# Differential attention: each unit's two weight tiles turned by products with diagonals of their factors and added in PSUM

## What is computed

```python
def diff_softmax_core(q, k, v, lam):
    s = jnp.einsum('bqhcd,bkhcd->bhcqk', q.astype(jnp.float32), k.astype(jnp.float32)) * (DA_HD ** -0.5)
    p = jax.nn.softmax(s, axis=-1)
    w = p[:, :, 0] - lam * p[:, :, 1]
    return jnp.einsum('bhqk,bkhe->bqhe', w, v.astype(jnp.float32))
...
    ax = diff_attn_latent(qx, jnp.concatenate([kc, kx], axis=1), jnp.concatenate([vc, vx], axis=1), lam)
...
    out_c = merge(diff_softmax_core(qc, kc, vc, lam), mc, pc[5]) if need_ctx else None
```

## Time and profile before

| | before |
|---|---|
| median of 3 runs | 2934.42 us |
| lowest, highest | 2933.34, 2937.86 us |
| the profiled execution's own time | 2933.31 us |
| its span, first to last instruction | 2931.3 us |
| outside the span | 2.0 us |
| mean granted TensorE clock | 0.983 |
| TensorE busy | 2828.8 us, 97% |
| VectorE busy | 2013.9 us, 69% |
| ScalarE busy | 1281.7 us, 44% |
| GpSimd busy | 339.3 us, 12% |
| chain that ended last | PE 80%, DVE 11%, ACT 5% |

### The profile page before, as it was taken

One profiled execution on the slowest core, in us unless ns is written; L12 is line 12 of the kernel. 1 busy time (PEld: TensorE's weight loads), 2 busy tenths in 40 slices (PEclk: granted clock), 3 DMA queues, 4 the chain that ended last, 5 costly groups with the idle time before them and its releaser, 6 DMA issues.

```text
span 2931.3 us, 44027 instructions
## 1 busy us (share of the span) xinstructions
PE 2828.8 (97%) x17694; PEld 2492.6 (85%) x17694; DVE 2013.9 (69%) x3397; ACT 1281.7 (44%) x2121; POOL 339.3 (12%) x380
## 2 busy tenths in 40 slices
PE   7999999998999999999999989999999999999998
PEld 6888898666888889888897889999979999887898
DVE  7789956555687656788655775666656689767764
ACT  4222244354422224222245565565455554645653
POOL 0000011322100001000011110022102210300100
PEclk8999999899999999999999999999999999999999
DMA  6666522011455534556432234455425579653453
GB/s 245 222 223 230 201 85 94 29 51 43 145 201 208 212 125 158 201 205 210 145 113 80 72 130 151 149 176 174 164 81 172 187 277 327 199 155 101 137 187 115
DMA packets 141194, 467.63 MB, mean 160 GB/s; under 512 B 27024, under 2 KB 29200, under 8 KB 140480
## 3 DMA queue, kind: packets, MB, share of 16 engines
q1 hardware_dynamic: 125440, 408.20, 41.2%
q0 software_dynamic: 15552, 56.63, 5.5%
HBM read 463.73 MB, written 1.05 MB: 159 GB/s over the span
## 4 chain that ended last, share of the span: by engine, by line
PE 80%; DVE 11%; ACT 5%; issue 2%; DMA 2%; POOL 1%; SPq 0%; ACTq 0%; DVEq 0%; POOLq 0%
PE bank L2657 24%; PE bank L2658 24%; PE bank L2659 24%; DVE sb_split_low L2061 3%; DVE sb_h_low L2148 1%; DMA sb_raw<-weights 1%; PE bank L2929 1%; PE bank L3100 1%; PE bank L2948 1%; DMA sb_ada_mlp<-ada 1%; DVE sb_temp L2075 1%; PE bank L2889 1%; DVE sb_x_res L2264 1%; DVE sb_temp L2142 1%; ACT sb_temp L1966 1%
## 5 line engine op out<-in xcount | busy, mean ns | idle before, releaser
L2657 PE MATMUL bank<-sb_h_high,sb_split_high 128*128 128x256 f32 (+1 forms) x3464 | 1116.6, 322 | 39.5 <-DVE sb_h_low L2156 16.5
L2658 PE MATMUL bank<-sb_h_low,sb_split_high 128*128 128x256 f32 (+1 forms) x3464 | 1097.8, 317 | 0.0
L2659 PE MATMUL bank<-sb_h_high,sb_split_low 128*128 128x256 f32 (+1 forms) x3464 | 1097.1, 317 | 0.0
L1646 ACT ACTIVATE sb_split_high<-sb_raw 128x1024 fp32r<-128x1024 f32 x620 | 646.4, 1051 | 306.6 <-PE bank L2659 286.2
L2061 DVE TENSOR_TENSOR sb_split_low<-sb_raw,sb_split_high 128x1024 fp32r<-128x1024 f32 x620 | 758.6, 1232 | 21.6 <-ACT sb_split_high L1646 21.5
L2657 PEld LDWEIGHTS bank<-sb_h_high,sb_split_high 128*128 128x128 f32 x3464 | 666.7, 192 | 100.9 <-issue 17.7
L2658 PEld LDWEIGHTS bank<-sb_h_low,sb_split_high 128*128 128x128 f32 x3464 | 667.8, 193 | 40.8
L2659 PEld LDWEIGHTS bank<-sb_h_high,sb_split_low 128*128 128x128 f32 x3464 | 667.0, 193 | 40.7
L2075 DVE CUSTOM_DVE_ANT_0 sb_temp<-sb_ada_ffn,sb_cond_ffn 128x1024 bf16<-128x1024 f32 x364 | 429.7, 1220 | 25.1 <-DMA sb_ada_ffn<-ada 16.0
L2657 PE MATMUL bank<-sb_hidden_high_ffn,sb_split_high 128*128 128x512 f32 (+1 forms) x830 | 280.4, 338 | 0.0
L2659 PE MATMUL bank<-sb_hidden_high_ffn,sb_split_low 128*128 128x512 f32 (+1 forms) x830 | 279.2, 336 | 0.0
(11 more groups left out here) (329 smaller groups left out, 3498.2 us busy)
## 6 DMA issues: line engine op xcount, KB each, us to landing
sb_raw<-weights SPq DMA_DIRECT2D x620, 512.0 KB, 3.4
sb_ada_ffn<-ada SPq DMA_DIRECT2D x114, 512.0 KB, 4.6
sb_ada_ffn<-ada POOLq DMA_DIRECT2D x90, 512.0 KB, 3.8
sb_ada_mlp<-ada POOLq DMA_DIRECT2D x18, 512.0 KB, 5.6
sb_ada_mlp<-ada SPq DMA_DIRECT2D x18, 512.0 KB, 5.9
sb_cond_ffn<-cond SPq DMA_DIRECT2D x3, 1024.0 KB, 5.4
sb_na_raw<-na_rpb SPq DMA_DIRECT2D x32, 96.0 KB, 6.8
sb_x_res<-tokens SPq DMA_DIRECT2D x4, 512.0 KB, 7.7
```

Of the source, the lines that this page charges most:

```text
L1646: do.activation(m.high[s % HIGHS][:, :], m.raw[s % RAWS][:, :], identity).then_inc(*act.mark("split_high", s))
L2657: do.matmul(out, ah, bh, start=start and j == 0, stop=False)
L2658: do.matmul(out, ah, bl, start=False, stop=False)
L2659: last = do.matmul(out, al, bh, start=False, stop=stop and j == len(terms) - 1)
```

## The change

`da_combine` is taken out of the list of steps, and `da_normalise` out of GpSimd's program. After the two factors, VectorE writes two diagonal matrices, the identity times factor 1 and the identity times factor 2, into two of six 128x128 places in `masks`. `da_turn` no longer transposes a combined tile: for each 128 keys it multiplies the first tile with the first diagonal and the second tile with the second one, and the two products are added in bank 3.

```diff
-    units = list(apart(turns(16, ("da_scores", "da_normalise", "da_combine", "da_turn"), more), "da_scores"))
+    units = list(apart(turns(16, ("da_scores", "da_normalise", None, "da_turn"), more), "da_scores"))
...
+    def da_diag(self, u, c):
+        at = (2 * (u % 3) + c) * P
+        return self.masks[:, at:at + P]
...
-    def da_normalise(u):
-        pool.wait_ge("exped", ("da", u, 1))
-        pool.wait_ge("recip", ("da", u))
-        first_scaled("da", u, m.cols[u % 6][:, 4:5])
...
         do.tensor_tensor(col[:, 5:6], col[:, 5:6], m.neg_lam[:, 0:1], ALU.mult).then_inc(*dve.mark("recip", ("da", u)))
+        dve.wait_ge("recip", ("da", u))
+        if u >= 3:
+            dve.wait_ge("turned", ("da", u - 3))
+        for c in range(2):
+            do.tensor_scalar(m.da_diag(u, c), m.C("ident"), col[:, 4 + c:5 + c], None, ALU.mult).then_inc(
+                *dve.mark("weights", ("da", u, c)))
...
-    def da_combine(u):
-        combine("da", u, m.cols[u % 6][:, 5:6])
...
     def da_turn(u):
-        pe.wait_ge("combined", ("da", u))
-        turn("da", u, 3, m.temp[2 * (u % 3)], even_keys(u))
+        nk = even_keys(u) // P
+        free(3)
+        for c in range(2):
+            pe.wait_ge("exped", ("da", u, c))
+            pe.wait_ge("weights", ("da", u, c))
+        for kt in range(nk):
+            for c in range(2):
+                last = do.matmul(m.bank[3][:, kt * P:(kt + 1) * P], m.temp[2 * (u % 3) + c][:, kt * P:(kt + 1) * P], m.da_diag(u, c),
+                                 start=c == 0, stop=c == 1)
+        last.then_inc(*pe.mark("turned", ("da", u)))
+        read[3] = "turn_copy", ("da", u)
```

More of the change, by code:

```diff
@@ L1591, in pool_program @@
     work = {"ada": ada, "square": square, "add_mean": add_mean, "centre": centre, "near_centre": near_centre,
-            "rope": rope, "da_normalise": da_normalise, "ml_normalise": ml_normalise, "even_norm": even_norm,
+            "rope": rope, "ml_normalise": ml_normalise, "even_norm": even_norm,
             "gla_decay3": gla_decay3, "gla_factors": gla_factors, "plain": plain}
@@ L2616, in vector_program @@
             "hidden_low": hidden_low, "add": add, "fm_copy": fm, "tm_copy": tm, "forget": forget, "lambda": lam,
-            "rope": rope, "conv": conv, "da_scores": da_scores, "da_normalise": da_normalise, "da_combine": da_combine,
+            "rope": rope, "conv": conv, "da_scores": da_scores, "da_normalise": da_normalise,
             "ml_weights": ml_weights, "ml_normalise": ml_normalise, "ml_combine": ml_combine, "even_stat": even_stat, "even_rstd": even_rstd,
```

## The result

The changed kernel took 2948.85 us in the median of 6 runs (2942.22 to 2954.76), the kernel before 2936.24 us in 6 runs beside them: +12.6 us, a ratio of 1.0046 with a 95% interval of 1.0033 to 1.0058. Two later jobs, each on another chip than the other, gave +8.8 us (1.0029, 1.0019 to 1.0040) and +12.8 us (1.0044, 1.0030 to 1.0059). The prediction was 2945.4 us, +11 us, slower with 0.90. It was right. The profiled execution happened to be the slowest of the six, 2954.76 us with a span of 2953.0, so its difference of 21 us to the one before has to be taken apart first. (The differences are of medians; the ratios are estimates of their own and not quotients of the medians, so the two can differ by 1 or 2 us.)

A forecast was written before the change was run, and what follows sets the result against it. TensorE was taken to bound the kernel, at 97% busy. Removed work 0, turnings and diagonals on the path +12.0 us, clock -1.0, gave +11 on 2934.42: 2945.4 us, range 2940 to 2951.5.

The forecast's parts named there:

- TensorE bounds the stretch, and what is removed is on nobody's path: Differential attention, 613 to 720 us: TensorE stage; removing 10.7 us of GpSimd scalings and VectorE combinings priced at 0.
- Added on TensorE, 15.4 us in all: Turning: 48 transposes become 96 fp32 products at 0.214 us; +0.64 us per context unit, +1.28 per latent unit.
- What lies on the path, 12.0 us at the clocks of before: Differential attention, unit by unit: added turning not hidden by TensorE stalls, plus diagonals delaying stall ends; +12.0 us.
- The turnings without a stall: Units 1, 2, 4, 7 (context) and 8, 9, 13, 14, 15 (latent): products follow without a gap; +9.0 us.
- units 0 and 3: Context units followed by stalls of 1.48 and 0.88 us: turning hidden, the pair of diagonals adds 0.5 us each.
- units 10, 11 and 12: Latent units: at 10 and 11 turning hidden, diagonals add 0.5 us each; at 12 the stall is no cover, +1.0.
- units 4 to 6: Context units: unit 4's turning fully on the path, +0.64 us; units 5 and 6 covered by stalls, 0.
- The clock, -1 us: Three half-clock stretches after TensorE's quiet times, 1.7 us each: somewhat under one expected to go, -1 us.
- The clock holds: Rival: TensorE stays at 2.4 GHz through all three stretches, returning 5.1 us; +6.9 us, 2940 to 2942; chance 0.18.
- All of it is serial: Rival: every turning and four pairs of diagonals lie on the path; +17.4 us, 2951.8; chance 0.13.
- a product costs four transposes: Rival: in the turnings a product takes 0.428 us; +26 us, 2961; chance 0.02.
- The signs of being wrong: Wrong if a product isn't 0.214 us, the clock falls at other places, or another stage moves by microseconds.

The follow-up runs named there:

- the variant on GpSimd: The changed kernel with each unit's two diagonals written by GpSimd instead of VectorE: 9.5 and 7.2 us above the kernel before, in two jobs.
- the unused diagonals: The kernel before, with VectorE also writing the 32 diagonals, which nobody reads, scaling and combining kept: 8.3 us above the kernel before, ratio 1.0030.
- the unused diagonals and a fill: The kernel before with VectorE's unread diagonals, plus three fp32 products of ones behind the turning of unit 0: 9.4 us above the kernel before.
- two products, GpSimd's diagonals and a fill: The changed kernel with diagonals on GpSimd, plus 1, 2 and 3 products of ones ahead of three 8-row groups: 5.4 us above the kernel before.

## Why the prediction was right

- *TensorE bounds the stretch, and what is removed is on nobody's path.* Right. GpSimd's 16 scalings and VectorE's 16 combinings are gone, and the idle time ahead of the reciprocal of the sums grew to 0.92 us in their place. Two kernels with 48 products each, the one by the identity with the scaling and the combining, the other by GpSimd's diagonals without them, have the same steps.
- *Added on TensorE, 15.4 us in all.* The form was right, the size a little low: a product takes 0.223 us, not 0.214, and a turning costs 0.72 and 1.36 us instead of 0.64 and 1.28. Why a product takes 4% more here than in the earlier trace rows isn't shown.
- *What lies on the path, 12.0 us at the clocks of before.* Right, unit by unit. Two profiles of the changed kernel have half-clock time of the same length in the same steps as the first profile of before, and their stretches are 12.7 and 12.8 us longer; the third has 14.3. The turnings without a stall gave 9.0 us over eight of them where 8.3 was forecast; units 0 and 3 gave 0.73 and 0.51 us instead of 0.5 each, shown to be the diagonals by the variant on GpSimd; units 10, 11 and 12 gave 0.57, 0.52 and 1.12 where 0.5, 0.5 and 1.0 was forecast; units 4 to 6 gave 0.3 in two profiles and 1.8 in one, where 0.64 was. So the stalls behind units 0, 3, 10 and 11 did take the turning in.
- *The clock, -1 us.* Not shown, neither size nor sign. The prediction read three quiet stretches with half clock behind them; the trace has 17.1 us of half clock in the stretch, and the longest piece, 6.8 us from 646.3 to 653.1, is missing from it. Measured against the first profile of before the changed kernel has the same 17.1 us, against the second 10.2 us less. Over all runs of the whole kernel the clock returned 4.0 us in one job (half of 8.0 ± 5.4) and took 0.5 in the other. That +11 stands so near to 12.6, 8.8 and 12.8 is due to the +12.0; within the spread that the clock gives, the last microsecond is luck.
- *The rivals.* "The clock holds" would have been +6.9 us by its own count, and +3.5 with the 17.1 us that there were (12.0 - 8.5). It did not hold: 17.1 us at half clock were left in each profile, 10.2 with the diagonals on GpSimd. The Trainium skill ("TensorE: Matmul & The Clock Gate", Part 4: PE-mode transpose) says that transposes count less for the clock than products; the kernel with products by the identity, where only that is exchanged, had 20.5 us at half clock, between 17.1 and 27.3 for transposes, and 4.9 us less over all runs with an interval of 6.2 each way: no run here shows it. "All of it is serial" at 17.4 us was not reached, since the stalls behind units 0, 3, 10 and 11 took the turning in. That a product costs four transposes (the Trainium skill, the same page, Terms, on the transpose mode for FP32) doesn't hold here: 1.78 us for eight against 0.43 for four is a ratio of 2.1 for each.
- *The signs of being wrong.* By their letter all three came up: a product isn't 0.214 us, the clock fell at other places in one profile, and the rest moved by 7 us in the first. The first was worth 0.7 us; the other two also differ between two executions of the kernel before, so they were set tighter than this kernel repeats.
- *What I didn't foresee.* The first profile was 21 us longer than before. Seven of these were low clock in stages which the change doesn't touch, and come and go between executions.

## What to carry to other kernels

Where TensorE is the bound, moving a scaling and an addition from engines with idle time into its products costs what the products cost: price them by a series of the same form and width, and take off only what falls into a stall whose end doesn't depend on them. Then look at what stood ahead of the waited-for result and what stands behind it: an operation of 10.7 us in sum was free because it lay in a wait, and its lighter successor was not, because it lay behind it. And in a kernel that loses time to a lowered clock, parts of a change don't add up: take the half-clock time of each profile off before comparing stages, compare steps that have the same of it, and multiply the span of every run by its mean clock, which here told cost from clock where medians and single profiles couldn't. An edit that isolates a part must also leave its neighbours as they are: the unused diagonals ran beside a scaling that the change removes, and took 446 ns instead of 284.

## What the runs showed of the hardware

- The clock's low times moved between executions of the same program: 45.8 and 49.6 us at half clock behind the stretch in two profiles of the kernel before, 60.1, 49.5 and 50.5 in three of the changed one; these made up to 7 us of the time, more than half of the change's effect.
- What is done in one stage changes how long the kernel runs at half clock, by more than chance between runs: over all runs of a job, 13.1 ± 4.4 us more than the kernel before with the unused diagonals and a fill, 17.5 ± 4.5 less with two products, GpSimd's diagonals and a fill. In one job the changed kernel had 8.0 ± 5.4 us less, and without its second product 10.6 ± 5.5 more. The kernels with VectorE's diagonals and few products have more of it, those with many products less; but the changed kernel in another job had 1.0 ± 4.6 more, and how much of the differences lies in the stage itself isn't shown.
- So a part can be cheap at full clock and dear in the runs: the unused diagonals cost 4.7 ± 1.8 us at full clock and 8.3 in the median, products by the identity 2.7 ± 1.6 and 0.5.
- The second of two 128x128 scalings on VectorE took 0.28 us with GpSimd idle, 0.50 while GpSimd scaled a 128x256 tile and 0.72 while it scaled a 128x512 one (the first, 0.29 in each case).
- The same 128x128 scaling took 284 ns on VectorE and 774 ns on GpSimd.
